# 4 instead of 22 context row products between key norm and query norm, two sum tiles in turn, and the context's second norm finished among tile 2's rows

## The reference

```
h = x * (1 + scale1) + shift1;  one projection h @ w_in gives HGRN2, attention and gate inputs
o_rec = bidirectional gated linear recurrence (8 heads)
o_att = grouped-query attention, q and k RMS-normed, rotary on latent tokens
y   = (sig(gA) * (o_rec @ w_branch_rec) + sig(gB) * (o_att @ w_branch_att)) @ w_out
x   = LayerNorm(alpha * x + gate1 * y)
x   = LayerNorm(alpha * x + gate2 * PEER(x * (1 + scale2) + shift2))
PEER(h): per token 8 heads x 16 experts of 16384, chosen by two top-16 lists of 128 keys each;
         a = gelu(u_tab[expert] . h);  out = sum over 128 (token, expert) pairs of gate * a * v_tab[expert]
```

## Time and profile before

| | us |
|---|---|
| median of 3 runs | 5685.8 (5678.53 to 5693.51) |
| the profiled execution | 5679.44 |
| its span, first to last instruction | 5677.5 |

### The profile page before, as it was taken

One profiled execution on the slowest core, in us unless ns is written; L12 is line 12 of the kernel. 1 busy time (PEld: TensorE's weight loads), 2 busy tenths in 40 slices (PEclk: granted clock), 3 DMA queues, 4 the chain that ended last, 5 costly groups with the idle time before them and its releaser, 6 DMA issues. The chain is left out here.

```text
span 5677.5 us, 60713 instructions
## 1 busy us (share of the span) xinstructions
PE 4544.5 (80%) x17704; PEld 2522.6 (44%) x17704; DVE 3716.1 (65%) x7024; ACT 1420.3 (25%) x3642; POOL 2230.4 (39%) x1826
## 2 busy tenths in 40 slices
PE   7889986889766777777788999868896767777776
PEld 6556653656433322222265566546563433222222
DVE  2367777857788766754533677778577887667545
ACT  2111212321011333333321122123210113433333
POOL 0012124641656454455400121246316564444564
PEclk9999997999988999999999999979998889999999
DMA  6755345785989999999957543557859889999998
GB/s 263 268 184 190 122 150 205 245 293 189 384 303 367 394 421 419 415 421 418 405 212 274 195 170 115 189 186 246 294 198 386 308 330 419 417 421 415 421 418 348
DMA packets 296659, 1705.84 MB, mean 300 GB/s; under 512 B 33424, under 2 KB 43280, under 8 KB 176272
## 3 DMA queue, kind: packets, MB, share of 16 engines
q0 software_dynamic: 258048, 1342.29, 61.3%
q1 hardware_dynamic: 23712, 338.18, 15.7%
q10 hardware_dynamic: 14576, 21.52, 1.0%
HBM read 1696.61 MB, written 5.24 MB: 300 GB/s over the span
## 5 line engine op out<-in xcount | busy, mean ns | idle before, releaser
L367 POOL DMA_INDIRECT arena<-in_peer_uv,eidx x1024 | 1221.5, 1193 | 1448.5 <-POOLq L366 1205.7
L2147 DVE SCALAR_TENSOR_TENSOR arena<-arena 128x1024 f32<-128x1024 f32 x384 | 470.7, 1226 | 355.8 <-DMA arena<-in_peer_uv,eidx 345.9
L410 POOL DMA_INDIRECT arena<-in_peer_uv,eidx x384 | 499.2, 1300 | 497.0 <-POOLq L409 476.4
L864 PE MATMUL banks<-arena 128*128 128x512 f32 x896 | 500.5, 641 | 238.7 <-PEq L1476 237.6
L837 PE MATMUL banks<-ring,arena 128*128 128x512 f32 x864 | 384.6, 600 | 113.4 <-PEq L819 113.4
L866 PE MATMUL banks<-arena 128*128 128x512 f32 x896 | 475.2, 613 | 0.0
L462 ACT ACTIVATE arena<-arena 128x1 f32<-128x1 f32 (+1 forms) x772 | 156.9, 203 | 1042.1 <-ACTq L461 1041.8
L467 ACT ACTIVATE arena<-ident,arena 128x128 f32<-128x128 f32 x832 | 333.7, 401 | 306.9 <-ACTq L466 305.1
L864 PEld LDWEIGHTS banks<-arena 128*128 128x128 f32 x896 | 154.0, 197 | 553.7 <-issue 553.2
L353 POOL COPY eidx<-arena 128x128 uint32<-128x128 uint32 x8 | 2.7, 341 | 987.5 <-POOLq L352 987.5
L2147 DVE SCALAR_TENSOR_TENSOR ring<-ring,arena 128x1024 f32<-128x1024 f32 x192 | 235.3, 1226 | 213.2 <-DMA ring<-in_peer_uv,eidx 212.3
(11 more groups left out here) (302 smaller groups left out, 7747.4 us busy)
## 6 DMA issues: line engine op xcount, KB each, us to landing
ring<-in_wblk SPq DMA_DIRECT2D x160, 2048.0 KB, 8.2
arena<-in_peer_uv,eidx POOLq DMA_INDIRECT x1408, 7.9
arena<-in_lnrows ACTq DMA_DIRECT2D x6, 1024.0 KB, 8.9
arena<-in_sk ACTq DMA_DIRECT2D x4, 1024.0 KB, 7.5
hT<-in_peer_uv,eidx POOLq DMA_INDIRECT x192, 14.1
ring<-in_peer_uv,eidx POOLq DMA_INDIRECT x192, 14.4
x<-in_x_sample ACTq DMA_DIRECT2D x1, 2048.0 KB, 28.9
out<-arena ACTq DMA_DIRECT2D x4, 512.0 KB, 7.3
```

Of the source, the lines that this page charges most:

```text
L367: nc.gpsimd.indirect_dma_start(grow[j], None, ins["peer_uv"], bass.IndirectOffsetOnAxis(ap=eidx[:, n, r:r + 1].bitcast(U32), axis=0)).then ...
L410: nc.gpsimd.indirect_dma_start(gslot[j], None, ins["peer_uv"].rearrange("(e h) d -> e (h d)", h=2), bass.IndirectOffsetOnAxis(ap=eidx[:, n ...
L864: nc.tensor.matmul(banks[:, b, :], diag[n], row[:, 0:CB], start=start, stop=stop, skip_group_check=True).then_inc(diag_used, 1)
L2147: V.scalar_tensor_tensor(u, u, 1.0, h2[:, t - 2, :], ALU.mult, ALU.mult, accum_out=av[:, r:r + 1])
```

## The change

- `HEAD_ROWS` is 8 instead of 6: levels 0 and 1 of each head carry two rows instead of one.
- `NORM_ROWS` is split: `KEY_ROWS` = 22 ahead of the key norm, `QUERY_ROWS` = 4 instead of 22 ahead of the query norm. 114 instead of 116 rows are done before attention; POOL issues 122 instead of 124 ahead. Attention's rowless units move from 6 and 7 to 7 and 8, its rows stay 124 in number, and `one_mix(one_tile)` has 18 rows (5, 5, 4, 4) instead of 16.
- Weighted sums go to two tiles in turn, `acc` for even rows and `sums[1]` for odd ones. The drain stands ahead of each even row only. `merge_sums()` adds them at the end (one 128x1024 addition), and two tiles are cleared instead of one. It holds for the context's sums and for `one_sum`.
- The context's second norm: part 0 stays in `one_mix(one_tile)`, parts 1 to 3 become pieces 27 to 29 of tile 2, that is behind slots 111, 115 and 119, with tile 2's gain and bias rows. ACT's square root for it moves from `one_mix` to slot 113 of tile 2, and the two `ln2c` loads go.

```diff
-HEAD_ROWS = 6
-NORM_ROWS = 44
+HEAD_ROWS = 8
+KEY_ROWS = 22
+QUERY_ROWS = 4
...
+        sums = [acc, arena[:, 28416:28416 + D]]
...
-        dots_end = GATE_ROWS + HEADS * HEAD_ROWS + NORM_ROWS
+        dots_end = GATE_ROWS + HEADS * HEAD_ROWS + KEY_ROWS + QUERY_ROWS
...
-                    if tl is one_tile:
-                        for n in range(2):
-                            act.dma_start(ln2c[n], ins["lnrows"][l, 2 + n].partition_broadcast(P)).then_inc(ln2_full, 16)
...
                         act.drain().then_inc(g2_ready, 1)
-                        square_root(1)
                     square_root(1)
...
-                        if r == 97:
+                        if r == 97 or (r == 113 and t == 2):
                             square_root(1)
...
+                def merge_sums():
+                    dve.drain()
+                    V.tensor_tensor(acc, acc, sums[1], ALU.add)
+                    dve.drain()
...
-                            V.scalar_tensor_tensor(acc, grow[j], wv[:, r - SLOTS:r - SLOTS + 1], acc, ALU.mult, ALU.add
-                                                   ).then_inc(row_free[j], 1)
-                            dve.drain()
+                            if r % 2 == 0:
+                                dve.drain()
+                            V.scalar_tensor_tensor(sums[r % 2], grow[j], wv[:, r - SLOTS:r - SLOTS + 1], sums[r % 2],
+                                                   ALU.mult, ALU.add).then_inc(row_free[j], 1)
...
-                        for part in range(4):
-                            second_norm(0, acc, bc2c, ln2c, part)
+                        merge_sums()
+                        second_norm(0, acc, bc2c, None, 0)
...
-                ctx_rows(NORM_ROWS // 2)
+                ctx_rows(KEY_ROWS)
...
-                ctx_rows(NORM_ROWS // 2)
+                ctx_rows(QUERY_ROWS)
...
+                    if t == 2 and 27 <= n < 30:
+                        second_norm(0, None, None, (ln2[:, 0, :], ln2[:, 1, :]), n - 26)
```

More of the change, by code:

```diff
@@ L220, in build @@
         bc2c = arena[:, 26624:27648]
-        ln2c = [arena[:, 27648:28672], h2c]
         yT = r3(arena[:, 23552:23552 + KD * GRP], GRP)
@@ L1871, in ctx_rows @@
                             V.tensor_tensor(wv, av, gates[0], ALU.mult)
-                            V.memset(acc, 0.0)
                             dve.drain()
+                            for part in sums:
+                                V.memset(part, 0.0)
                         dve.wait_ge(row_full[j], rows_landed(l, r // SLOTS, r % SLOTS))
@@ L1914, in one_mix @@
                         dve.sem_inc(g2_ready, -1)
-                        dve.wait_ge(ln2_full, 32)
-                        dve.sem_inc(ln2_full, -32)
-                        for part in range(4):
-                            second_norm(0, acc, bc2c, ln2c, part)
+                        merge_sums()
+                        second_norm(0, acc, bc2c, None, 0)
                     t = tl.t
@@ L2163, in one_sum @@
                         dve.wait_ge(row_full[j], rows_landed(l, 3, r))
-                        V.scalar_tensor_tensor(acc, grow[j], wv[:, r:r + 1], acc, ALU.mult, ALU.add
+                        if r % 2 == 0:
+                            dve.drain()
+                        V.scalar_tensor_tensor(sums[r % 2], grow[j], wv[:, r:r + 1], sums[r % 2], ALU.mult, ALU.add
                                                ).then_inc(row_free[j], 1)
-                        dve.drain()
                 def mix(n):
```

## The result

The changed kernel takes 5729.5 us (median of 4, 5721.06 to 5736.9) against 5682.9 for the kernel before (4 runs): ratio 1.0079, 95% interval 1.0064 to 1.0094. It is slower by 0.8%, 45 to 47 us. 5618 had been forecast, with 0.04 for slower. The profiled execution has a span of 5725.7 us against 5677.5.

The account below looks back on a forecast made before the run. DVE was taken to set the pace in heads, norms and half of attention's units, DMA in tile 2. From 5679.4 us, -62.7 - 5 + 36.7 - 28 - 4.6 + 2.6 = -61.0 gave 5618, range 5590 to 5652.

Parts of the forecast that it names:

- Rows out of the norms: Query norm: four rows from full buffers instead of 22, saving 62.7 us; PE's projections the next bound, not yet reached.
- Warm start: After the norms: PE pauses 3 us, not 33, so first scores run at the higher clock; -5 us over two layers.
- Rows into the heads: Latent heads: two more rows in each of sixteen heads, 1.15 us each, paid in full; +36.7 us over two layers.
- Drains in attention: Attention: undrained sums shorten DVE-paced units and may lift PE's clock; -14 us a layer, -28 in all.
- The unit: Attention: a unit paced by DVE takes 3.31 us instead of 3.60, in four of a pair's eight units.
- the middle gap: PE's gap in the middle of an attention pair, 1.75 us, was expected near 1.2.
- the middle dip: PE's low clock behind an attention pair's middle gap; if gone, -19.6 us a layer instead of -7.9; the middle was taken.
- the gap at the pair's end: PE's 2.80 us gap ending an attention pair, held too long to vanish by half a microsecond.
- Norm moved: Context's second norm leaves `one_mix`: gain 0, since DVE waits for PE instead; ACT's table load joins the chain, +2.6 us.
- Drains in tile 1's sum: Tile 1's sum: rows at 1.29 instead of 1.377 us, less merge and clearing; -4.6 us over two layers.
- rival 5: Attention and tile 1's sum: undrained sums shut POOL out, DVE waits for rows; +54 us, 5733; chance 0.04.
- Rival 1: Attention and tile 1's sum: an undrained sum is as slow as a drained one; -24 us, 5655; chance 0.10.

Follow-up runs that it names:

- attn_drained: `sum_drained` with the drain also ahead of every weighted sum of the context's rows, two tiles kept; 5663.3 us, 0.9952 of the kernel before.
- sum_drained: Changed kernel with a drain ahead of every row of tile 1's sum instead of every second; 5647.3 us, 0.9924 of the kernel before.
- sum_only: Kernel before with the edit of tile 1's sum alone (two tiles, drain ahead of even rows, one merge); 5792.8 us, 1.0169.
- sum_short_row: Changed kernel with rows 8 to 95 of tile 1's sum gathered at 128 of 1024 columns; 5744.1 us, 1.0096 of the kernel before.
- pool_break: Changed kernel with four tiny drained GpSimd memsets after every eighth gather issued for tile 1's sum; 5783.8 us, 1.0161 of the kernel before.
- sum_paced: Changed kernel with a one-column VectorE memset behind every second row of tile 1's sum; 5709.4 us over 10 runs, 1.0034 of the kernel before.
- wait_first: Changed kernel with both waits for a pair's rows ahead of the pair in tile 1's sum; 5684.8 us over 10 runs, 0.9998 of the kernel before.

## Why the prediction was wrong

Step by step, in the order of its sum (two layers):

- *Rows out of the norms, -62.7.* Right: from the query rows' start to the query norm 31.05 and 31.96 us less, -63.0. The bound that was named, PE's projections, wasn't reached.
- *Warm start, -5.* Measured 0 in layer 0 and +0.8 in layer 1: the clock had fallen within the pause of 2.23 us that was left.
- *Rows into the heads, +36.7.* From the first multiplication of a level to the last, 337.5 to 355.3 and 336.9 to 354.9 us: +35.7. Right; the clock is still 0.99 and 0.98 over the heads.
- *Not in the sum.* VectorE waits 2.1 and 1.6 us more for PE between the heads and the key rows, and in layer 1 the 24 rows ahead of the heads take 3.8 more. With these the stretch to the first score minimum gained 18.7, not 31.
- *Drains in attention, -28.* Measured -22.7 in the two traces; by runs, `attn_drained` to `sum_drained`, -16. The unit and the middle gap are right to 0.05 us, and the middle dip went everywhere, where I had given it half. What I missed is that the gap at the pair's end now weighs more.
- *Norm moved, +2.6.* The waits and the table load are as told. By runs nothing is measurable; the 5.1 and 2.9 us that the stretch lost in the changed kernel's trace are not there in `sum_drained` (459.6 / 456.8), which has the same norm.
- *Drains in tile 1's sum, -4.6, bounds -13 to +4.6 for both layers.* This is the step that failed: measured +96 (traces +97, `sum_only` +96). Its own terms hold (1.284 a row, the merge 1.22). What fails is the path: I costed DVE's rows and DMA's share and put TensorE at nothing, since its four blocks, which ended 53 us ahead of the sum in the kernel before, seemed safe cover. Beside the undrained rows they took 175 us instead of 97, and the choice waited 66 us for them. No rival and no bound of mine had TensorE late there.

The measured 5729.5 lies by rival 5's 5733, but not by its mechanism. That rival had GpSimd shut out by undrained sums, attention slower and rows at 1.62. The runs show the opposite: attention is faster, and GpSimd issues every 1.29 us. It had the right place and the right two engines, VectorE without drains and GpSimd, and the wrong victim.

Rival 1, too, is out: sums of a pair start 1.20 apart, and the drained start of the next pair comes 1.37 behind. Of the Trainium skill, page "VectorE: DVE Perf Modes", section "The DRAIN you can't avoid", the prediction gave the rule that the next operation does not start until the pipe is empty; by it alone they would have been as slow as drained ones, and the trace disagrees. It left out the section's own exception, that a next operation which is not held starts earlier, and with that one the trace agrees. The Trainium skill, page "SBUF — State Buffer", section "Who interferes with whom", says that DMA never contends with a compute engine; `sum_short_row` agrees, since PE was held back alike at 50 and at 410 GB/s. What does hold it remains unnamed.

No row of the kernel before shows TensorE held back beside the sum, but its trace could have warned: GpSimd's issues stood 1.377 apart there, and the closest in any trace stand 1.24 apart. The edit took away most of the slack of an engine that I had only asked whether it would keep up.

## What to carry to other kernels

When an edit lets one engine run faster, list every engine that works beside it in that stage, TensorE too, and ask of each what slack it had; one that is "only cover" can turn into the bound. Take a drain out one place at a time and time each place: here it gave 16 us in attention and cost 82 to 96 in a loop that reads the same. Check every layer and every repeat of a stage before calling a kernel free of a trouble: `sum_drained` is free in layer 0 and held back in layer 1, and its time alone doesn't tell. And where PE's rows have long gaps marked "issue", look at when the engine that takes its results gets going; that told here that matmuls were late, not missing.

## What the runs showed of the hardware

- TensorE can be slowed to one instruction per 1.40 us (a weight load and a matmul per 2.80) for 30 us and more, with no wait in its program and "issue" as the only name in the profile; its matmuls are on record up to 74 us ahead of their semaphore. It came in all eight kernels with undrained pairs of `scalar_tensor_tensor` on VectorE beside long runs of gathers 1.24 to 1.34 us apart, from some 10 to 12 gathers in, and in layer 1 of three kernels without such pairs, from 15 to 22 gathers in.
- A gather of 128 rows costs GpSimd 1.24 to 1.34 us, with rows of 512 bytes as with 4 KB; a drain of GpSimd behind eight of them kept it for 4 to 10 us (`pool_break`).
- Two weighted sums of 128x1024 start 1.20 us apart without a drain and 1.377 with one. A one-column memset ahead of a drain costs nothing (2.58 against 2.57 a pair).
- TensorE's granted clock read 1.00 up to 908 us and 0.57 over 908 to 912, behind 27.7 us of matmuls, ten transposes and a pause of 2.23 us.
- `sum_paced` and `wait_first` scatter by 68 us from run to run, where the kernel before scatters by 13 to 21.
